# Shorter clock keeping and rounded copies first before the attention, and attention outputs kept channel-major and scaled in PSUM

## The reference, cut to what matters

```
q = h @ q_w                       # 16 heads of 64 channels
k, v = h @ kv_w                   # read by the attention only
sc = q k^T / 8 + bias             # 256 tokens, causal, window per head group
pr = exp(sc - max);  den = sum(pr)
o = (pr v) / den                  # per head
w_g = 3 * softmax over the 3 head groups of mean(log(den) + max)   # per token
mix = concat(o of group g * w_g) @ o_w
h = layer_norm(alpha * h + mix)   # then the experts
```

## Time and profile before

| | |
|---|---|
| median of 3 runs | 1221.58 us |
| the profiled execution's own time | 1217.74 us |
| its span, first to last instruction | 1215.8 us |
| TensorE busy | 1180.0 us, 97% |
| VectorE, ScalarE, GpSimd busy | 37%, 28%, 18% |
| granted TensorE clock, mean | 0.995 |
| HBM read | 424.69 MB, 351 GB/s over the span |
| first mixture of experts | about 205 to 685 us |
| attention with its projections | 694 to 819 us |
| second mixture of experts | 828 to 1208 us |

### The profile page before, as it was taken

One profiled execution on the slowest core, in us unless ns is written; L12 is line 12 of the kernel. 1 busy time (PEld: TensorE's weight loads), 2 busy tenths in 40 slices (PEclk: granted clock), 3 DMA queues, 4 the chain that ended last, 5 costly groups with the idle time before them and its releaser, 6 DMA issues.

```text
span 1215.8 us, 17555 instructions
## 1 busy us (share of the span) xinstructions
PE 1180.0 (97%) x6510; PEld 691.7 (57%) x6510; DVE 454.6 (37%) x893; ACT 335.5 (28%) x572; POOL 213.6 (18%) x111
## 2 busy tenths in 40 slices
PE   8999999999999999999999899999999999999995
PEld 6997777544454455544444488885445444544442
DVE  3776774532222222222222534455222222222234
ACT  5579962111111111111110355602111111111110
POOL 2466874100000000000000487321000000000000
PEclk9999999999999999999999999999999999999998
DMA  9723447999999999999999832579999999999991
GB/s 370 280 105 139 173 162 310 372 403 430 429 427 429 429 428 428 430 427 429 429 429 426 332 108 101 190 299 385 399 430 428 429 429 427 429 428 428 429 426 73
DMA packets 34534, 427.09 MB, mean 351 GB/s; under 512 B 3664, under 2 KB 5872, under 8 KB 8000
## 3 DMA queue, kind: packets, MB, share of 16 engines
q1 hardware_dynamic: 32064, 416.12, 82.1%
q10 hardware_dynamic: 2240, 9.66, 2.2%
q0 software_dynamic: 192, 0.79, 0.2%
HBM read 424.69 MB, written 1.87 MB: 351 GB/s over the span
## 4 chain that ended last, share of the span: by engine, by line
PE 87%; DVE 8%; ACT 2%; issue 1%; DMA 1%; POOL 1%; ACTq 0%; SPq 0%; DVEq 0%
PE bank L783 34%; PE bank L845 17%; PE bank L766 9%; PE bank L691 3%; PE bank L939 3%; PE bank L555 3%; PE bank L830 3%; PE bank L831 2%; PE bank L937 2%; PE bank L1010 1%; DVE arena L1510 1%; DVE arena L1558 1%; PE bank L672 1%; PE bank L816 1%; PE bank L741 1%
## 5 line engine op out<-in xcount | busy, mean ns | idle before, releaser
L783 PE MATMUL bank<-ring,arena 128*64 128x512 f32 x928 | 409.9, 594 | 0.0
L492 POOL TENSOR_TENSOR split_ring<-ring,split_ring 128x1024 fp32r<-128x1024 f32 x56 | 138.4, 2500 | 488.2 <-ACT split_ring L485 481.7
L845 PE MATMUL bank<-reach_down,arena 128*64 (+1 forms) x464 | 206.0, 595 | 2.2 <-DVE arena L1716 2.2
L845 PE MATMUL bank<-ring,arena 128*64 128x512 f32 x464 | 205.8, 596 | 0.0
L783 PE MATMUL bank<-reach_up,arena 128*64 (+1 forms) x464 | 205.5, 595 | 0.0
L783 PE MATMUL bank<-reach_gate,arena 128*64 (+1 forms) x464 | 205.4, 593 | 0.0
L783 PEld LDWEIGHTS bank<-ring,arena 128*64 128x64 f32 x928 | 124.0, 137 | 131.4 <-issue 126.1
L1732 DVE TENSOR_TENSOR arena<-arena,bank 128x512 f32<-128x512 f32 x116 | 72.3, 683 | 168.5 <-PE bank L831 168.5
L766 PE MATMUL bank<-arena 128*128 128x128 f32 x928 | 115.5, 277 | 0.7 <-DVE arena L1810 0.7
L766 PEld LDWEIGHTS bank<-arena 128*128 128x128 f32 x928 | 108.2, 192 | 2.3 <-issue 2.3
L845 PEld LDWEIGHTS bank<-reach_down,arena 128*64 128x64 f32 x464 | 60.8, 136 | 83.3 <-issue 80.1
(11 more groups left out here) (277 smaller groups left out, 1456.3 us busy)
## 6 DMA issues: line engine op xcount, KB each, us to landing
reach_gate<-in_gate_w SPq DMA_DIRECT2D x29, 2048.0 KB, 16.8
reach_up<-in_up_w SPq DMA_DIRECT2D x29, 2048.0 KB, 20.9
reach_down<-in_down_w SPq DMA_DIRECT2D x29, 2048.0 KB, 19.0
ring<-in_gate_w SPq DMA_DIRECT2D x27, 2048.0 KB, 15.8
ring<-in_up_w SPq DMA_DIRECT2D x27, 2048.0 KB, 16.6
ring<-in_down_w SPq DMA_DIRECT2D x27, 2048.0 KB, 13.8
ring<-in_in_w SPq DMA_DIRECT2D x9, 2048.0 KB, 21.3
ring<-in_out_w SPq DMA_DIRECT2D x4, 2048.0 KB, 8.8
```

What stands on the lines that cost most here:

```text
L492: unit.tensor_tensor(split_ring[:, j % RING, here], ring[:, j % RING, here], split_ring[:, (j + 1) % RING, here], ALU.subtract).then_inc(d ...
L783: last = mm(bank[out_bank][64 * e:64 * e + 64, :], exT[:, k, 64 * e:64 * e + 64], w, start=k == 0, stop=k == KD - 1)
L845: last = mm(bank[5 + c][64 * e:64 * e + 64, :], hidT[:, k, 64 * e:64 * e + 64], w, start=k == 0, stop=k == 3)
```

## The change

Four things, all around the attention:

- `keep_clock(8, 2)` becomes `keep_clock(5, 2)`, and `keep_clock(3, 6)` becomes `keep_clock(1, 6)`.
- In `copy_hT` ScalarE makes the four rounded copies first and the four full ones behind them; VectorE subtracts for banks 5, 7, 4, 6. `project(0)` and `project(1)` are cut in two: both units' first two products, then both units' third.
- `values(m)` works on a pair of heads: `v` is the weight operand (64 channels, so a half of the array's columns for each head of the pair), the turned probabilities move (256 and 128 columns), and the output has channels in rows, which is what `o_block` reads. No output has to be turned.
- The weights of the heads are turned instead: ScalarE spreads the 16 numbers of a token over 1024 columns (`spread`, 128x2048), TensorE turns that by 16 transposes into banks 4 to 7 (`spread_weights`), and VectorE multiplies there, in PSUM, by the unscaled outputs (`scaled`). ScalarE copies the outputs (`o_copy`) and takes all four high parts (`oT_round`), VectorE all four low parts (`oT_rest`). `spread` takes the place of `lnw`, so that the load of the next norm's rows moves behind the transposes.

```diff
-            keep_clock(8, 2)
+            keep_clock(5, 2)
             normed()
...
-            for kind, n in ATT_ORDER:
+            def values(m):
+
+                projected(UNIT_OF_V[m // 4])
+                pe.wait_ge(att["ptc"], 2 * m + 2)
+                if m >= 4:
+                    pe.wait_ge(att["oc"], m // 2 - 1)
+                b, c, p = bank[2 + m // 2 % 2], m % 2 * S, pT[m]
+                for i in range(2):
+                    at = (2 * m + i) * HD
+                    mm(b[HD * i:HD * i + HD, c:c + S], v[:, 0, at:at + HD], p[:, i, 0:S], start=True, stop=False,
+                       skip_group_check=True)
+                for i in range(2):
+                    at = (2 * m + i) * HD
+                    mm(b[HD * i:HD * i + HD, c + P:c + S], v[:, 1, at:at + HD], p[:, i, S:S + P], start=False,
+                       stop=True, skip_group_check=True).then_inc(att["pv"], 1)
+
+            def spread_weights():
+
+                pe.wait_ge(att["wexp"], 2)
+                for m in range(8):
+                    for t in range(TB):
+                        c = m % 2 * S + t * P
+                        last = nc.tensor.transpose(bank[4 + m // 2][:, c:c + P],
+                                                   spread[:, t, m * P:(m + 1) * P], ident)
+                    if m % 2:
+                        last.then_inc(att["oT"], 1)
+
+            project(0, (0, 1))
+            project(1, (0, 1))
+            project(0, (2,))
+            project(1, (2,))
+            for kind, n in ATT_ORDER[2:]:
...
-            for n in range(8, 12):
-                values(n)
-            token_transposes(pe, osb, range(4), att["oT"], att["o"])
-            for n in range(12, AH):
-                values(n)
+            spread_weights()
+            for m in range(4, 8):
+                values(m)
...
             for k in range(4):
                 o_block(k, (0,))
-            token_transposes(pe, osb, range(4, KD), att["oT"], att["o"])
+            pe.wait_ge(att["oc"], 4)
             for k in range(4):
                 o_block(k, (1,))
...
-            keep_clock(3, 6)
+            keep_clock(1, 6)
...
             def copy_hT():
 
-                for i in (0, 2):
-                    act.wait_ge(hT_mm, 4 + i + 1)
-                    for k in (2 * i, 2 * i + 1):
...
+                for rounded in (True, False):
+                    for i in (0, 2):
+                        act.wait_ge(hT_mm, 4 + i + 1)
+                        for k in (2 * i, 2 * i + 1):
+                            g, b = C_LNG + KD + k, C_LNB + KD + k
+                            last = A((aT_high if rounded else hT)[:, k, :], bank[4 + i][:, (k % 2) * S:(k % 2 + 1) * S],
+                                     ACT.Identity, scale=cst[:, g:g + 1], bias=cst[:, b:b + 1])
+                        last.then_inc(hT_a, 1)
...
+            def oT_round(i):
+
+                act.wait_ge(att["o"], i + 2)
+                A(oT_high[:, 2 * i:2 * i + 2, :], bank[4 + i][:, :].rearrange("p (k s) -> p k s", k=2),
+                  ACT.Copy).then_inc(att["oTa"], 1)
...
+            act.wait_ge(att["o"], 1)
+            act.wait_ge(h_ready, 2)
+            A(spread.rearrange("p t (h c) -> p t h c", c=HD), am[:, 8, :, :].unsqueeze(3).to_broadcast([P, TB, AH, HD]),
+              ACT.Copy).then_inc(att["wexp"], 1)
+            high_chunks(4)
+            oT_round(0)
+            oT_round(1)
+            act.wait_ge(att["oT"], 4)
             load_ln(2)
             load_ln(3)
-            high_chunks(4)
...
+            o_copy(2)
+            o_copy(3)
+            oT_round(2)
+            oT_round(3)
...
-                for i in range(4):
+                for i in (1, 3, 0, 2):
...
+            def scaled(i):
+
+                dve.wait_ge(att["oT"], i + 1)
+                dve.wait_ge(att["oc"], i + 1)
+                b = bank[4 + i][:, :].rearrange("p (k s) -> p k s", k=2)
+                product(b, o_raw[:, 2 * i:2 * i + 2, :], b).then_inc(att["o"], 1)
...
-            scaled_heads(8)
...
+            for i in (0, 2):
+                scaled(i)
+                scaled(i + 1)
+                oT_rest(i)
+                oT_rest(i + 1)
```

More of the change, by code:

```diff
@@ L509, in logit_bank @@
             return 5 if L == 0 else 0
-        def token_transposes(pe, src, tiles, done, halves):
-            for k in tiles:
-                if k % 4 == 0:
-                    pe.wait_ge(halves, k // 4 + 1)
-                for t in range(TB):
-                    b = bank[4 + k // 2]
-                    c = (k % 2) * S + t * P
-                    last = nc.tensor.transpose(b[:, c:c + P], src[:, t, k * P:(k + 1) * P], ident)
-                if k % 2:
-                    last.then_inc(done, 1)
         @block.tensor
@@ L939, in project @@
                             last = mm(bank[u % 2][:, 0:S], w[:, k, (n % 4) * P:(n % 4 + 1) * P], a[:, k, :], **ends)
-                last.then_inc(att["proj"], 1)
+                if 2 in products:
+                    last.then_inc(att["proj"], 1)
                 if last_use:
```

78 lines of the change are left out of this document (21 added, 57 removed).

## The result

| | before | changed |
|---|---|---|
| median of the runs | 1220.8 us | 1214.18 us |
| ratio, 95% interval | | 0.9938 (0.9919 to 0.9958) |
| the profiled execution's own time | 1217.74 us | 1215.47 us |
| its span | 1215.8 us | 1213.4 us |
| TensorE busy | 1180.0 us | 1177.1 us |

Faster by 0.6%, about 7.6 us where 3.7 were forecast. One of the eight runs of the changed kernel took 4163.11 us, at a granted clock of 1.00; the ratio leaves it out, and no profile shows why. The median of 1214.18 lies at the lower edge of the range, near rival 1's figure (1214.7), but what ran was not rival 1, as the rows show.

The account below looks back on a forecast made before the run. TensorE was taken to bound the attention, so that gains there reach the end. Terms of -0.1, +0.6, -2.1, -1.7 and -0.4 sum to -3.7 us, taking the median from 1221.58 to 1217.9 us, range 1214.0 to 1221.3.

Parts of the forecast that it names:

- rival 1: Before the projections, all four subtractions pass ahead of GpSimd, or the cast is not held: 1214.7 us, chance 0.27.
- The stall on the subtractions: In the first projections, TensorE waits 3.8 us for VectorE's subtractions, held by GpSimd's chunks.
- The -0.1: Ahead of and in the first projections: fewer dummies, reordered copies and TensorE's wait together give -0.1 us.
- The clock's term: Around the first projections: a clock fall in TensorE's new wait costs +0.6 us, between 0 and 1.7.
- The covers: Ahead of the attention: with five dummies, the first tile's eight transposes fill TensorE's time while the second is normalised.
- Values: In the attention loop: a pair of heads takes 0.75 us instead of 1.28; four pairs give -2.1 us.
- Rival 3: In the value products: the two array halves don't overlap, values gain nothing; +0.2 us, 1221.8 us, chance 0.07.
- The prediction's other estimate: In the value products: 0.81 us a pair, from the skill's 2.38 times for three column tiles; term -1.9 us.
- Behind the last projection: From the last projection on: `o_block` starts earlier and its eight transposes go; -1.7 us, between +0.1 and -2.0.
- Clock keeping, 3 to 1: In the router stretch: with two dummy records for six, TensorE waits for the second normalised tile; -0.4 us.
- Rival 2: Behind the last projection and before the last turn: two clock falls, up to 1.7 us each; 1221.3 us, chance 0.12.
- a sign that is to prove a case: At the first projection: running through without a wait was to prove that the subtractions or the cast went free.

Follow-up runs that it names:

- e9: The changed kernel unedited, measured and profiled once more: 0.9946 of the kernel before.
- e13: The changed kernel with one useless VectorE instruction of 128 columns ahead of the subtractions: 0.9989 of the kernel before.
- e14: The changed kernel with one useless VectorE instruction of 256 columns ahead of the subtractions: 0.9979 of the kernel before.
- e5: The changed kernel with GpSimd's second chunk held until the four subtractions are done: 0.9955 of the kernel before.
- e6: The changed kernel with eight subtractions of 256 columns in place of four of 512: 1.0016 of the kernel before, 1223 us.
- e7: The changed kernel with units 0 and 1 projected one after the other, without the split: 0.9976 of the kernel before.
- e1: The kernel before with only the dummies ahead of the attention cut from eight to five: 1.0002 of the kernel before.
- e15: The changed kernel with two useless VectorE instructions of 256 columns ahead of the subtractions: 0.9989 of the kernel before.
- e16: A repeat of the changed kernel with VectorE rounding straight from PSUM: 0.9955 of the kernel before.
- e8: The changed kernel with VectorE rounding straight from PSUM and writing the unrounded tiles afterwards: 0.9947 of the kernel before.
- e12: The changed kernel with a pair's four value products issued head by head instead of alternating: 0.9943 of the kernel before.

## Why the prediction was wrong, step by step

**The stall on the subtractions is the step that failed:** "So GpSimd takes its turn behind the second". It took it behind the third. The subtractions started 3.56 us behind ScalarE's first copy (695.24 less 691.68) and not 3.87, since GpSimd's chunk held the first cast to 693.95, 0.6 us and not 0.9. GpSimd's next was issued 4.79 us behind it (4.78 forecast), 0.08 us behind the end of ScalarE's first copy of a weight chunk, as in every profile but those that hold the chunk back. The margin to the third subtraction was 0.03 us, and 0.01 to 0.03 in all eight profiles with this landing (e9 among them), so the landing recurs. That it fell on the good side of so small a margin was luck as far as the forecast goes. So the wait was 1.13 us in e9 and not 3.8: 2.35 for one chunk fewer and 0.3 for the earlier start. The -0.1 becomes -2.8, which is what A shows. e13 and e14 show the forecast's case, with a landing behind the second subtraction: two are held, TensorE waits, and A is 2.4 us longer, the price of one chunk. So the mechanism was right, its place on the clock was not, and the sum should have carried both landings as cases of equal standing.

**Rival 1 is not what ran.** Its 1214.7 us is near the measured time by luck. Its term of -2.65 does not follow from the bullets above it either: without the wait of 3.8 us the -0.1 becomes -3.9, and e9 less its wait of 1.13 is at -4.0. With the subtractions free and the clock fallen, A was -2.8 (e5).

**The clock's term did not come.** I had +0.6 for a fall in the new wait. In the first profile the half clock stretched 26 matmuls over the wait and cost nothing (22.12 against 22.04 in A), and the wait of 1.13 us in e9 brought no fall. The longer waits of e6 (7.84 us) and e7 (3.02 us) did, in e7 for 2.2 us (12.10 for 9.87). This is the other 0.6 of the 3.3 us by which A was missed. The kernel before has no such wait, so there the fall costs 1.3 us when it comes (12.77 for 11.47; I had read 1.7 from the stretches). Part of what the changed kernel gains is that it no longer pays this.

**The covers held, nearly:** the five dummies ended at 690.42, ahead of the second tile's normalisation (done at 691.15 in that profile), and the first tile's transposes filled the time, as the prediction had it. The 16 transposes took 2.04 us for 1.91, so 0.1 us was lost. The cast was held. I gave the rounded-first order nearly nothing, and 0.1 us is what e1 shows for it at the start of the last pair. What the prediction did not price is the split: without the order and the split the dummies' gain is lost (e1, 1.0002), and without the split alone most of it (e7, 0.9976 for 0.994).

**Values:** 0.80 us in the loop where I took 0.75, and 0.65 in the row of four, the 0.64 of perfect halves. Four pairs of 0.48 are 1.9; B got 1.5 to 1.6. Part of the rest is in the turns of the probabilities behind the values: from 746.67 to the next scores it is 0.81 us, for 0.76 from 749.31 before, and 0.2 us over all eight. The projections between account for about as much again. Rival 3 is out. The prediction's other estimate, 0.81 us, fits a pair in the loop (0.80) and is too long for one in a row (0.65).

**Behind the last projection:** -1.9 for -1.7, `o_block` 6.0 us behind it for 6.1.

**Clock keeping, 3 to 1:** -0.35 where the clock held, as forecast. Rival 2 came in one of its two places, with 3.1 us (D 16.30 for 13.18) in seven of the twelve profiles with two records, where its chance was 0.12 for both. The other place, behind the last projection, did not: the granted clock stayed at 1.00 through 0.92 us of waiting and the 16 transposes of 786.34. The Trainium skill, page "TensorE: Matmul & The Clock Gate", section "Part 4: PE-mode transpose", says that a transpose "doesn't count as PE-busy the same way". Here they did no harm alone. In the first profile the fall came behind a wait of 1.14 us and eight transposes, while the 40-column products ran; five profiles had the same instructions there, the same wait and no fall.

**The total:** -6.6 in an execution without the fall in D, -3.5 in one with it. The measured -7.6 and -6.6 us (0.9938 and 0.9946) lie nearer to the first, and their difference is within the intervals. What share of unprofiled executions has the fall can be guessed only: in the first measurement the three runs with a mean granted clock of 0.994 to 0.996 took 1209.2 to 1210.3 us, and the four with 0.990 to 0.992 took 1213.5 to 1215.6, the profiled one among them. The mean does not say where the clock fell.

**What stays open:** why a chunk sometimes goes next and sometimes waits for the whole queue. It went next at 0.01 to 0.31 us into a subtraction (ten profiles) and waited at 0.32 to 0.34 (e15, e16, e8; 0.60 us is the subtractions' own pace). But e13's 0.31 and e15's 0.32 are the same within the rounding of the rows, and in e6 a chunk issued 0.1 us ahead of the next subtraction went first. So the place within a subtraction does not settle it alone, and no experiment here separates what does.

## What to carry to other kernels

When an edit moves one engine against another that can hold it up, work out the landing to 0.1 us, and if it is nearer than that to a boundary, forecast two cases. Put work of the bottleneck engine between a product and the operand that comes last (the split: some 4 us), because it covers a late operand and a fallen clock alike. Dummies that look idle in one profile may hold the clock in the next: judge them over several profiles. And check a sign that is to prove a case for other ways to come about: the first projection ran through, and it was the fallen clock that hid the wait.

## What the runs showed of the hardware

- Between a VectorE subtraction with two SBUF operands and a GpSimd operation, strict turns are kept over four rounds (e6). The Trainium skill, page "SBUF — State Buffer", section "Who interferes with whom", says that a VectorE instruction with two SBUF inputs contends with a GpSimd instruction that reads SBUF, and that whoever issues first gets the ports that they share for its whole instruction (the latter it says of VectorE's two-port modes). The changed kernel's rows agree (697.04 behind 696.47, held); e8, e15 and e16 don't: subtractions issued 0.26 to 0.28 us behind GpSimd's chunk, and all behind them, went first.
- The granted clock falls in some executions of the same instructions and not in others. In the first 160 us, which no edit touches, it was 0.96 over the first 40 us in eleven of 18 profiles and 0.87 over 120 to 160 us in four. That moves all that follows: the first dummy stood at 683.75 in e8, with neither, and at 691.40 in e15, with both. That this makes most of the spread between unprofiled runs is likely, not shown. Around the first projections it fell in 13 of 18: in ten of the eleven with the early fall and in three of the other seven.
- Two products on the two column halves of TensorE overlap in full at 256 and 128 columns, in whichever order they are issued: 0.65 us a pair in a row (e12 and the changed kernel), where 0.64 is what full overlap costs by the 0.43 us of a 512-column record.
